# The modulation product of a two-block transformer kernel: weights fetched as rows of 2048 columns, four sums at once in column tiles of TensorE

## The reference, cut to what matters

```python
mod = jax.nn.silu(c) @ ada_w[layer] + ada_b[layer]          # c: 1 x 2048, ada_w: 2048 x 6144
shift, scale, gate = jnp.split(mod, 3, axis=-1)
h = rms_norm(x, norm_g[layer]) * (1.0 + scale[:, None, :]) + shift[:, None, :]
proj = h @ w_in[layer]                                       # all else of block one, then block two
```

## Time and profile before

| what | value |
| --- | --- |
| median of 3 runs | 2075.23 us |
| lowest and highest of the runs | 2074.75 and 2078.66 us |
| span of the profiled execution | 2077.4 us |
| TensorE busy, over the span | 2028.5 us (98%) |
| VectorE, ScalarE, GpSimd busy | 1321.0, 923.7 and 382.8 us |
| read from HBM | 404.31 MB |

### The profile page before, as it was taken

One profiled execution on the slowest core, in us unless ns is written; L12 is line 12 of the kernel. 1 busy time (PEld: TensorE's weight loads), 2 busy tenths in 40 slices (PEclk: granted clock), 3 DMA queues, 4 the chain that ended last, 5 costly groups with the idle time before them and its releaser, 6 DMA issues.

```text
span 2077.4 us, 23555 instructions
## 1 busy us (share of the span) xinstructions
PE 2028.5 (98%) x9213; PEld 1603.7 (77%) x9213; DVE 1321.0 (64%) x1684; ACT 923.7 (44%) x1218; POOL 382.8 (18%) x588
## 2 busy tenths in 40 slices
PE   6989999999999999999999999999999999999999
PEld 1268787777887878777788888888888888878887
DVE  4867667899676669878975665644445444444443
ACT  1155523455654544354554434544444444433332
POOL 0000001999999960000000000000000000000000
PEclk9999989999999999999999999999999999999999
DMA  9977656655566675554446555556556565555654
GB/s 339 350 255 240 211 192 202 203 174 168 177 209 205 199 209 184 177 164 159 152 129 203 190 187 183 183 189 196 182 187 197 183 194 191 191 166 190 199 187 161
DMA packets 206242, 407.93 MB, mean 196 GB/s; under 512 B 10874, under 2 KB 12979, under 8 KB 205491
## 3 DMA queue, kind: packets, MB, share of 16 engines
q1 hardware_dynamic: 190480, 376.07, 54.9%
q10 hardware_dynamic: 13892, 23.88, 3.5%
q0 software_dynamic: 1760, 6.49, 1.6%
HBM read 404.31 MB, written 2.10 MB: 196 GB/s over the span
## 4 chain that ended last, share of the span: by engine, by line
PE 74%; POOL 18%; DMA 3%; DVE 3%; issue 2%; ACTq 0%; ACT 0%; SPq 0%; DVEq 0%; POOLq 0%
PE ps L430 45%; PE ps L437 22%; POOL proj L2314 17%; PE pm L518 4%; DMA raw<-in_ada_w 2%; PE ps L518 1%; POOL h3T L2314 1%; DVE mod_part L1159 1%; PE pm L530 1%; POOL proj L2293 1%; PE pm L893 0%; DVE raw_lo L408 0%; DMA proj<-in_z 0%; PE pm L582 0%; DMA rows_b<-in_hgrn_norm_g 0%
## 5 line engine op out<-in xcount | busy, mean ns | idle before, releaser
L408 DVE TENSOR_TENSOR raw_lo<-raw,w_hi 128x1024 fp32r<-128x1024 f32 (+1 forms) x648 | 799.4, 1236 | 568.1 <-ACT w_hi L399 558.8
L399 ACT ACTIVATE w_hi<-raw 128x1024 fp32r<-128x1024 f32 (+1 forms) x648 | 680.4, 1051 | 802.4 <-PE ps L437 775.0
L430 PE MATMUL ps<-w_hi,h_hi 128*128 128x512 f32 (+1 forms) x2336 | 938.0, 402 | 3.9 <-DVE h_lo L975 3.0
L430 PE MATMUL ps<-w_hi,h_lo 128*128 128x512 f32 (+1 forms) x2336 | 912.3, 391 | 0.0
L437 PE MATMUL ps<-raw_lo,h_hi 128*128 128x512 f32 (+1 forms) x2336 | 627.3, 391 | 8.3 <-DVE raw_lo L408 8.3
L430 PEld LDWEIGHTS ps<-w_hi,h_hi 128*128 128x128 f32 x2336 | 442.7, 190 | 105.0 <-issue 9.8
L437 PEld LDWEIGHTS ps<-raw_lo,h_hi 128*128 128x128 f32 x2336 | 439.4, 189 | 104.1 <-DVE raw_lo L408 12.3
L430 PEld LDWEIGHTS ps<-w_hi,h_lo 128*128 128x128 f32 x2336 | 443.1, 190 | 94.0 <-issue 7.4
L2314 POOL TENSOR_TENSOR proj<-proj 128x128 f32<-128x128 f32 x264 | 184.1, 702 | 12.9
L430 PE MATMUL ps<-w_hi,hid_hi 128*128 128x512 f32 x256 | 100.6, 393 | 0.0
L430 PE MATMUL ps<-w_hi,hid_lo 128*128 128x512 f32 x256 | 100.3, 392 | 0.0
(11 more groups left out here) (322 smaller groups left out, 1147.6 us busy)
## 6 DMA issues: line engine op xcount, KB each, us to landing
raw<-in_w_in SPq DMA_DIRECT2D x140, 1024.0 KB, 5.2
raw<-in_w_ffn_gate SPq DMA_DIRECT2D x44, 1024.0 KB, 5.2
raw<-in_w_ffn_up SPq DMA_DIRECT2D x44, 1024.0 KB, 5.1
raw<-in_w_ffn_down SPq DMA_DIRECT2D x44, 1024.0 KB, 5.1
raw<-in_ada_w SPq DMA_DIRECT2D x32, 1024.0 KB, 7.7
raw<-in_w_out SPq DMA_DIRECT2D x32, 1024.0 KB, 5.1
proj<-in_ada_w ACTq DMA_DIRECT2D x16, 1024.0 KB, 5.2
raw<-in_w_br_hyena SPq DMA_DIRECT2D x8, 1024.0 KB, 5.1
```

The source lines that it names most:

```text
L399: nc.scalar.activation(w_hi[:, p % HRING, :, 0:gm.width(j)], raw[:, k % RING, e:e + HT, 0:gm.width(j)], ACT.Copy).then_inc(hi_done, 1)
L408: nc.vector.tensor_tensor(raw_lo[:, k % RING, e:e + HT, 0:gm.width(j)], raw[:, k % RING, e:e + HT, 0:gm.width(j)], w_hi[:, p % HRING, :, 0 ...
L430: nc.tensor.matmul(ps[pair][:, t, 0:gm.width(j)], l[:, tok], hi[:, i, 0:gm.width(j)], start=(k == 0 and l is x_hi), stop=False)
```

## The change

The stage takes another shape. A load now takes, from each partition, one k and one half of the 4096 columns: a single piece of 2048 columns. There are 32 of them again, of 1 MiB each. The four blocks of 512 columns in a load add into four rows of one PSUM bank, rows 0, 32, 64 and 96, of `mod_sums` (`ps[0]`), half 0 and half 1 in one bank each. TensorE multiplies all of it, so all 4096 sums stay open until the end. VectorE clears the two banks once, and does `before_products` in one piece. At the end ScalarE copies bank 0 and VectorE bank 1 (128 x 512 each) to `mod_rows`, and eight transposes of 128 x 128 turn them into `ps[1]`, from which VectorE picks one column in 32. The turns of the small vectors (`turn_vectors`) move behind the fourth load.

```diff
+H1_TURNED = (17, 21, 25)
@@ tensor
             pe.wait_ge(sig("c_silu"), 1)
-            for g in range(n_ada):
-                pe.wait_ge(sig("mod_read"), g + 1)
-                for c in (0, 2, 3):
-                    pe.wait_ge(landed[c], 16 * (g + 1))
-                    for k in range(CK if c < 3 else ADA_PE):
-                        m = mm(ps[g % 2][0:1, 0, :], c_sig[:, CK * c + k:CK * c + k + 1], raw[:, c, k],
-                               start=(c == 0 and k == 0), stop=False)
-                    m.then_inc(ada_used, 1)
-                pe.wait_ge(mod_parts, 2 * g + 2)
-                mm(ps[g % 2][0:1, 0, :], ones[:, 0:1], mod_part[:, g % 2], start=False, stop=True).then_inc(sig("mod_sum"), 1)
...
+            pe.wait_ge(sig("sums_clear"), 1)
+            for i in range(2 * KT):
+                k, half = i // 2, i % 2
+                pe.wait_ge(landed[i % RING], 16 * (i // RING + 1))
+                for q in range(CK):
+                    m = mm(mod_sums[CHUNK // 2 * q:CHUNK // 2 * q + 1, half, :], c_sig[:, k:k + 1], raw[:, i % RING, q],
+                           start=(k == 0), stop=(k == KT - 1), skip_group_check=True)
+                m.then_inc(ada_used, 1)
+                if i == RING - 1:
+                    turn_vectors()
+                if i in H1_TURNED:
+                    pe.wait_ge(sig("h1_rows"), 1)
+                    turn_unit("h1", hbuf, H1_TURNED.index(i))
+            for half in range(2):
+                pe.wait_ge(sig(f"mod_read{half}"), 1)
+                for q in range(CK):
+                    m = nc.tensor.transpose(mod_turns[:, half, q * P:q * P + P], mod_rows[:, half, q * P:q * P + P], ident[:])
+                m.then_inc(sig("mod_turned"), 1)
@@ vector
+            v.memset(mod_sums[:], 0.0).then_inc(sig("sums_clear"), 1)
...
-                    early.step(g, 2.5)
-            early.rest()
+            for _ in before_products():
+                pass
+            dve.wait_ge(ada_used, 2 * KT)
+            v.tensor_copy(mod_rows[:, 1], mod_sums[:, 1]).then_inc(sig("mod_read1"), 1)
@@ scalar
-            for g in range(n_ada):
-                act.wait_ge(sig("mod_sum"), g + 1)
-                s.activation(mod_row[0:1, g * GW:g * GW + GW], ps[g % 2][0:1, 0, :], ACT.Copy).then_inc(sig("mod_read"), 1)
...
+            act.wait_ge(ada_used, 2 * KT - 1)
+            s.activation(mod_rows[:, 0], mod_sums[:, 0], ACT.Copy).then_inc(sig("mod_read0"), 1)
             for n in range(2):
                 high(act, g_in, 0, n)
@@ sync
-                for c in range(RING):
-                    ada_free(sp, g, c)
-                    sp.dma_start(raw[:, c], ada_v[:, CK * c:CK * c + CK, GW * g:GW * g + GW]).then_inc(landed[c], 16)
+            for i in range(2 * KT):
+                k, half = i // 2, i % 2
+                if i >= RING:
+                    sp.wait_ge(ada_used, i - RING + 1)
+                sp.dma_start(raw[:, i % RING].rearrange("p k n -> p (k n)"), ada_v[:, k, D * half:D * half + D]).then_inc(landed[i % RING], 16)
```

More of the change, by code:

```diff
@@ L243, in build @@
         st = ExitStack()
-        mod_row = sb("mod_row", [P, 2 * D], F32, st)
-        mod_part = sb("mod_part", [P, 2, GW], F32, st)
+        mod_rows = sb("mod_rows", [P, 2, GW], F32, st)
         st.close()
@@ L381, in stream @@
                     if k < RING:
[L382 removed]
+                        sp.wait_ge(ada_used, RING * (n_ada - 1) + k + 1)
                     else:
@@ L562, in _, with turn_vectors @@
[L562 to L565, removed]
+            def turn_vectors():
+                pe.wait_ge(sig("rows_in"), 16 * 11)
+                pe.wait_ge(sig("rows_clear"), 3)
+                for key, t_, n in (("ra", rows_a, P), ("rb", rows_b, P)):
+                    nc.tensor.transpose(bank(pe, key, "v")[:, 0:n], t_[:], ident[:]).then_inc(filled, 1)
+                nc.tensor.transpose(bank(pe, "w1", "v")[:, 0:EMB], w1_rows[:], ident[0:EMB, 0:EMB]).then_inc(filled, 1)
@@ L1147, in _ @@
             dve.wait_ge(sig("c_silu"), 1)
-            early = Spare(before_products())
-            for g in range(n_ada):
[L1150 to L1166, removed]
-                    early.step(g, 2.5)
-            early.rest()
-            dve.wait_ge(sig("mod_turned"), 1)
-            link(v.tensor_tensor(mod_cols[:], mod_bank[:, 0:2 * KT], cols[:, C_AB:C_AB + 2 * KT], ALU.add))
+            for _ in before_products():
+                pass
+            dve.wait_ge(ada_used, 2 * KT)
+            v.tensor_copy(mod_rows[:, 1], mod_sums[:, 1]).then_inc(sig("mod_read1"), 1)
+            for half in range(2):
+                dve.wait_ge(sig("mod_turned"), half + 1)
+                k = slice(KT * half, KT * half + KT)
+                link(v.tensor_tensor(mod_cols[:, k].rearrange("p (q j) -> p q j", q=CK),
+                                     mod_turns[:, half].rearrange("p (j q r) -> p q j r", j=CK, q=CK)[:, :, :, 0],
+                                     cols[:, C_AB + KT * half:C_AB + KT * half + KT].rearrange("p (q j) -> p q j", q=CK), ALU.add))
             link(v.scalar_tensor_tensor(g_col[:], mod_cols[:, KT:2 * KT], 1.0, cols[:, C_NORM:C_NORM + KT], ALU.add, ALU.mult))
@@ L1890, in _ @@
                 squares("h1", j)
[L1891 to L1898 removed]
+            root("h1")
+            act.wait_ge(sig("lb_less"), 2)
+            s.activation(lb, lb, ACT.Exp).then_inc(sig("lb_exp"), 1)
+            act.wait_ge(ada_used, 2 * KT - 1)
+            s.activation(mod_rows[:, 0], mod_sums[:, 0], ACT.Copy).then_inc(sig("mod_read0"), 1)
             for n in range(2):
```

30 lines of the change are left out of this document (1 added, 29 removed).

## The result

The changed kernel takes 2061.72 us (median of four runs, 2060.07 to 2065.48). The kernel before, run beside it, takes 2074.99 us (median of four, 2074.1 to 2078.66). The ratio is 0.9934, with a 95% interval of 0.9918 to 0.995. The forecast was 2060.5 us in a range of 2055 to 2070. The span of the profiled execution is 2060.1 us, where 2062.7 was forecast. The forecast of the span was worked from one profile of the kernel before, and the experiments show how far one profile can lie from the next.

What follows compares the result with a forecast made beforehand. TensorE's matmul row was taken as fixed, so the first product's start decides: 110.3 - 9.0 (gaps) - 4.5 (pieces) = 96.8, plus 7.6 = 104.4 us, 14.7 sooner. 2075.2 - 14.7 = 2060.5 us, range 2055 to 2070.

Steps and rivals of the forecast that it cites:

- The bound: Whole kernel: TensorE's row of matmuls keeps its length, so only the first product's start, at 119.13 us, can move.
- The sums: Modulation stage: a load's four matmuls overlap in column tiles, 0.9 to 1.0 us, or 1.9 us at 1.2 GHz.
- The rival in which the sums don't overlap: Modulation stage: TensorE paces it at 3.42 us a load, start at 129 us, 2085 us in all; chance 4%.
- The ring: Slots for `ada_w` loads: freed soon enough that the drops in DMA rate close, winning 9.0 us.
- The pieces of 8 KB: Loads of `ada_w`: larger pieces move at 410 GB/s instead of 389, 2.56 us a load, winning 4.5 us over 32.
- The last landing: End of the `ada_w` loads: the last piece lands at 96.8 us instead of 110.3.
- The tail: Last `ada_w` piece to first product: 7.6 us, if `mod_ready` comes within 4.7 us; its chain takes 3.3 to 4.6.
- Nothing: Modulation stage: clearing two banks, `before_products` in one piece, and the turns of small vectors and x cost no time.
- part of the gain: Rival: gaps partly stay, 8 KB pieces no faster, or low clock persists; start 113.2 us, 2069.3 us; chance 18%.

Runs made afterwards that it cites:

- the second measurement: The changed kernel again with no edit, timed beside the kernel before: median of six runs 2065.79 us, ratio 0.9944.
- the third profile: The changed kernel with no edit, profiled once more: first product at 101.61 us, rest 1956.6 us, this run 2060.33 us.

## Why the prediction was right, point by point

**The bound** held. In the profiles the gain is the moment of the first product, and the rest stayed as long as it was, in eight of them.

**The sums** were forecast at 0.9 to 1.0 us a load and 1.9 at the low clock, and took 1.04 and 1.88. Full overlap of four would be one matmul's step and the tail of its record, 0.86 + 0.17 = 1.03 us; of two, 2 x 0.86 + 0.17 = 1.89, and the experiment with two tiles shows 1.88. So the rate gained is 4 and 2 within the trace's precision. The Trainium skill (TensorE: Matmul & The Clock Gate, Measured speedup vs the span model) gives less for three tiles, 2.38 times. By an estimate from its efficiency of 0.79, four sums would take 3.42/3.2 + 0.17 = 1.24 us with the record's tail, and the trace has 1.04.

**The rival in which the sums don't overlap** is the experiment with one tile. Start 128.1 where the rival said 129, and 2085.5 us where it said 2085. Its condition wasn't met, and its working was right but for one term: it gave 5 us for the low clock of the first loads, where the first 32 records take 16.13 us and would take 13.9 at 0.43 a step, so 2.2 us.

**The ring**: the gaps were to give 9.0 us. With 2 KB pieces, that is with the gaps closed and nothing else, the last landing is at 101.49; the prediction's own sum has 110.3 - 9.0 = 101.3. It was worked from the 110.3 us of one profile, though, and the kernel before has 108.4 and 107.7 in its second and third, so against a usual execution the gaps give 6 to 9 us. In the third it isn't even the last landing that ends the stage: TensorE's sums run on without a wait from 101.8 to 111.5 us.

**The pieces of 8 KB** is the term that was mis-sized. I took 410 GB/s, 0.14 us a load and 4.5 us in all. It is 421, 0.22 us a load, and 6.9 us. Of the values considered I stayed near 405, because the profile before had shown 8 KB rows only in a mixed queue without overlap. The upper bound of 425 was nearer, though not for its reason: packets hardly overlap at 8 KB (share 100.9%), they are moved faster: 7.56 MB in 100.9% of 18 us are 416 GB/s of engine time, where the prediction read 405 while x landed. A bound from a queue's share in a stretch that other queues share is a weak one.

The Trainium skill (DMA: Bandwidth & Descriptors, Measured) has 425 GB/s for one core's transfer of 16 MB; here loads of 1 MiB queued behind one another reach 421, close to it. The Trainium skill (DMA: Bandwidth & Descriptors, Where 436 GB/s comes from) also has a limit of some 358 GB/s on the memory's side that binds such loads; here the trace is above it at every size of piece, with 387 at the least.

**The last landing** came at 94.6 us and not 96.8; the 2.2 us between are the piece term's 2.4 less 0.2 of the gap term.

**The tail** of 7.6 us is 102.22 - 94.62 = 7.60. `mod_ready` was to come 3.3 to 4.6 us after the last landing, and 4.7 was the point from which it would cost; it came after 4.24, with the last sums at the low clock, in 1.73 us. The cover is thin: `g_col` at 98.86 and the second split at 99.35.

**Nothing**: the first 17 us, `before_products` and the turns cost nothing as forecast. One thing did move that I hadn't named: the load of the bounds lands only near 65 us, 31.7 us after its issue (10.3 before), and VectorE waits 19.6 us for it. It still has its work done well ahead of the last landing.

**The clock.** The rival "part of the gain" feared that a low clock might stay as the product begins. Some profiles begin their first product at the low level (0.79 us for its first record) and some at the high one (0.50), with starts and rests alike. It can't be seen in the time.

**Luck.** The forecast of 2060.5 us lies 1.2 us from the measured median, and that is closer than the working deserves. Two errors cancel. The stage gained more than forecast, 16.9 us between the first two profiles or 15.9 between means, and not 14.7. The timed median fell by less, 13.3 us, and in the second measurement, with a median of 2065.79, by 9.4. The pieces' share is the term of the sum that was wrong; that the medians move less than the start wasn't in the prediction at all.

**What stays open.** The starts are 16 us apart and the rests alike, which should give 16 us. The timed medians give 13.3 and 9.4. With 2 KB pieces it is the same, 8.7 us of start and 4.9 of time. Several executions of the changed kernel without a profile take 2064.5 to 2067.75 us, more than any of its five profiled ones (2059.9 to 2062.2). Whether their stage or their rest is longer wasn't seen. Their mean granted clocks are 0.971 to 0.976, mostly lower than the 0.976 to 0.978 of nearly all the short ones, which would fit more dips behind the start. But the third profile has 0.973 and takes 2060.33 us, since its low clock lies in the stage (PEclk 0.62 there, 0.69 in the first), so the mean clock can't settle it. The kernel with one tile, in which DMA doesn't set the pace, starts 10.3 us later than the kernel before and takes 10.3 us longer, and three of its four runs lie within 0.2 us of each other. That hints at the reading of `ada_w` but shows nothing.

## What to carry to other kernels

Where a full TensorE and a full DMA queue take turns in a stage, look at GB/s by stretch: the drops tell who paces, and taking away the slot's user (here by column tiles) wins the drops and no more. Vectors times wide matrices can run as two or four sums in column tiles at once. Once DMA paces the stage, the piece that each partition reads is the next lever, then the bytes that the stage doesn't need; but a load that is moved brings its work along, and behind the start VectorE had little room for it. And profile the kernel before more than once: its stage alone scattered over 2.2 us, which is more than some terms of the sum.

## What the runs showed of the hardware

- Four float32 matmuls with one stationary and 512 moving columns each, in column tiles at rows 0, 32, 64 and 96, with different operands, take 1.04 us together at 2.4 GHz. In two tiles they take 1.88, and in one tile they go one after another, 19 records in 8.32 us or 0.86 us a matmul.
- One core's loads from memory, with 16 engines busy: 387, 409 and 421 GB/s in pieces of 2, 4 and 8 KB, each partition's pieces 384 KiB from the next one's.
- A granted clock at 1.2 GHz over most of a stage costs nothing where DMA paces it: start 102.1 us at PEclk 0.69 and 101.9 at 0.96.
- I hadn't expected the clock of the long product row to differ between executions of one program. It dips to 1.2 GHz at much the same places, 22.5 us in all in one profile and 34 to 40 us in eight others, and the rest then takes 1951.5 or 1955.6 to 1958.3 us. That is 4 us or more, 0.2%, as much as some changes are worth.
